# Feed-forward stage of a two-block transformer kernel: the root's product back in the turns, and ScalarE's queue reordered around it

## The reference, cut to what matters

```
h = rms_norm(x, g)                      # x * 1/sqrt(mean(x^2)) * g
gu = h @ w_in                           # 1024 -> 2 * 2816
f = (silu(gu[..., :2816]) * gu[..., 2816:]) @ w_out      # 2816 -> 1024
```

## Time and profile before

| | us |
|---|---|
| median of 3 runs (lowest, highest) | 1759.24 (1759.04, 1760.07) |
| the profiled execution, its own time | 1758.46 |
| span of the profiled execution | 1756.6 |
| matrix engine busy in it | 1684.0 (96%) |
| VectorE, ScalarE, GpSimd busy | 1008.4, 735.9, 678.0 |

### The profile page before, as it was taken

How to read it: one execution, slowest core, us unless ns; L and a number is a source line. 1 busy time by engine, 2 the same in 40 slices (tenths; PEclk the granted TensorE clock), 3 DMA queues, 4 the chain that set the end, 5 groups by cost and what they waited for, 6 DMA issues and landing times.

```text
span 1756.6 us, 25803 instructions
## 1 busy us (share of the span) xinstructions
PE 1684.0 (96%) x8873; PEld 1387.2 (79%) x8877; DVE 1008.4 (57%) x1652; ACT 735.9 (42%) x1187; POOL 678.0 (39%) x308
## 2 busy tenths in 40 slices
PE   9999999999999984999999999999999989996799
PEld 7888777787899974888788766778889879995687
DVE  6744875657767773208497676642234786767113
ACT  7333554434433333327524676542224433333222
POOL 2444222444454423444343003534444344451443
PEclk9999999999999997999999999999999999998899
DMA  5344211222333221234332111122333223331232
GB/s 201 129 146 140 95 61 49 84 88 80 107 98 107 96 96 60 86 106 134 133 96 72 49 49 49 49 83 89 99 101 97 85 83 97 96 103 53 84 97 71
DMA packets 47642, 162.36 MB, mean 92 GB/s; under 512 B 5724, under 2 KB 7900, under 8 KB 47304
## 3 DMA queue, kind: packets, MB, share of 16 engines
q1 hardware_dynamic: 43440, 150.70, 27.1%
q10 hardware_dynamic: 4120, 10.59, 1.8%
HBM read 156.91 MB, written 4.76 MB: 92 GB/s over the span
## 4 chain that ended last, share of the span: by engine, by line
PE 42%; issue 38%; POOL 14%; DVE 3%; ACT 1%; DMA 1%; POOLq 0%; SPq 0%; DVEq 0%; ACTq 0%
POOL w_lo L500 14%; PE ps L584 11%; PE ps L585 11%; PE ps L586 11%; PE ps L1275 1%; PE ps L1274 1%; PE ps L1276 1%; PE ps L824 1%; PE ps L842 1%; PE ps L868 1%; PE ps L1172 1%; PE ps L1131 1%; PE ps L1153 1%; PE ps L1100 1%; DMA hT<-xT 1%
## 5 line engine op out<-in xcount | busy, mean ns | idle before, releaser
L500 POOL TENSOR_TENSOR w_lo<-w_raw,w_hi 128x1024 fp32r<-128x1024 f32 x260 | 638.8, 2463 | 954.1 <-ACT w_hi L1357 927.3
L1357 ACT ACTIVATE w_hi<-w_raw 128x1024 fp32r<-128x1024 f32 x271 | 284.1, 1054 | 350.4 <-PE ps L586 240.5
L584 PE MATMUL ps<-u_hi,w_hi 128*128 128x512 f32 x984 | 403.9, 410 | 6.3 <-POOL w_lo L500 6.1
L586 PE MATMUL ps<-u_hi,w_lo 128*128 128x512 f32 x984 | 385.0, 391 | 0.0
L585 PE MATMUL ps<-u_lo,w_hi 128*128 128x512 f32 x984 | 385.0, 391 | 0.0
L584 PEld LDWEIGHTS ps<-u_hi,w_hi 128*128 128x128 f32 x984 | 185.6, 189 | 51.9 <-issue 8.5
L586 PEld LDWEIGHTS ps<-u_hi,w_lo 128*128 128x128 f32 x984 | 185.3, 188 | 40.0
L585 PEld LDWEIGHTS ps<-u_lo,w_hi 128*128 128x128 f32 x984 | 185.8, 189 | 36.9 <-issue 1.4
L584 PE MATMUL ps<-a_hi,w_hi 128*128 (+1 forms) x264 | 105.0, 398 | 52.1 <-POOL w_lo L500 52.1
L585 PE MATMUL ps<-a_lo,w_hi 128*128 (+1 forms) x264 | 104.2, 395 | 0.0
L586 PE MATMUL ps<-a_hi,w_lo 128*128 (+1 forms) x264 | 104.2, 395 | 0.0
(11 more groups left out here) (455 smaller groups left out, 3594.8 us busy)
## 6 DMA issues: line engine op xcount, KB each, us to landing
w_raw<-stream SPq DMA_DIRECT2D x277, 512.0 KB, 3.5
g_rep<-g_one ACTq DMA_DIRECT2D x1, 2560.0 KB, 14.1
spread<-m_rows ACTq DMA_DIRECT2D x4, 512.0 KB, 4.2
tmp<-tmp ACTq DMA_DIRECT2D x32, 64.0 KB, 2.6
bias<-g_rep ACTq DMA_DIRECT2D x1, 2048.0 KB, 9.3
outT<-hT SPq DMA_DIRECT2D x13, 128.0 KB, 1.8
hT<-xT SPq DMA_DIRECT2D x3, 512.0 KB, 7.4
mem_in<-memT ACTq DMA_DIRECT2D x1, 1024.0 KB, 5.3
```

What stands on the lines that cost most here:

```text
L500: pool.tensor_tensor(w_lo[:, slot], w_raw[:, slot], w_hi[:, slot].bitcast(F32), ALU.subtract)\
L584: pe.matmul(out, wh, xh, start=start, stop=False)
L586: return pe.matmul(out, wl, xh, start=False, stop=stop)
L1357: act.activation(w_hi[:, slot], w_raw[:, slot], ACT.Copy).then_inc(hi_ready, 1)
```

## The change

1. **The root's product goes back into the turns.** `rooted` is gone. `plain_mid` multiplies in place and then by `rs`; `fast_up` has a product by `rs` between its two others. `plain_up` and `fast_up` raise `fast_a` themselves.
2. **The tail on ScalarE.** Eight roundings, feed 8, six roundings, feed 9, the last gate, seven roundings, feed 10 (the third down unit's), the last rounding. `down_act` then no longer feeds that unit, and the memory norm's squares stand behind the feeds of the next six.
3. **The tail on VectorE.** `a_lo` tiles in groups of four between the last gate, mid and up steps.
4. **In a turn on VectorE,** `sums_low(i, 3)` stands before `plain_gate`, not behind it.
5. **The first pairs.** ffn1 on VectorE: all four T tiles first, then the first gate, the weight sums, the rest of the pair, `sums_low`, the second pair. On ScalarE: the feeds of f + 3, f + 4 and f + 5 stand between and behind the T tiles, `sums_hi` before the second gate, and the feeds of f + 6 and f + 7 behind it. ffn2 on VectorE: weight sums ahead of pair 3 and `sums_low` ahead of pair 4; ScalarE's queue to match.

```diff
 # turn(i, last) on ScalarE
-                        for k in range(2):
+                        for k in range(8):
                             split(k)
                         feed_at(i, 8)
-                        for k in range(2, 6):
+                        for k in range(8, 14):
                             split(k)
                         feed_at(i, 9)
                         gate(LAST_E_BANK)
-                        for k in range(6, FT):
+                        for k in range(14, FT - 1):
                             split(k)
+                        feed_at(i, 10)
+                        split(FT - 1)
...
 # down_act
-                feed_after(u)
+                if half:
+                    feed_after(u)
                 if u + 10 + AHEAD < UNITS:
-                    with act.Fori(0, 3) as i:
+                    with act.Fori(0, 2) as i:
                         for j in range(R):
                             feed_loop(u + 1, j, i, R)
+                    if squares:
+                        squares()
+                    for j in range(7, 10):
+                        feed_after(u + j)
...
 # one_turn (ffn1): ScalarE's first turn
                 root("n_ffn", T)
                 feed_after(u + 1)
+                t_tile(2)
+                feed_after(u + 2)
+                t_tile(3)
                 sigmoids()
                 gate()
-                feed_after(u + 2)
-                t_tile(2)
-                t_tile(3)
                 feed_after(u + 3)
+                sums_hi(0, 0)
                 gate()
                 feed_after(u + 4)
-                sums_hi(0, 0)
                 feed_after(u + 5)
                 gate()
...
 # two_turns (ffn2)
                 t_tile(0)
                 t_tile(1)
-                gate()
                 feed_after(u + 8)
-                t_tile(2)
-                t_tile(3)
-                gate()
                 gate()
                 feed_after(u + 9)
+                t_tile(2)
                 feed_after(u + 10)
+                t_tile(3)
                 sums_hi(0, 0)
                 gate()
                 feed_after(u + 11)
+                gate()
+                gate()
...
 # plain_mid on VectorE
-                    step(dve.tensor_tensor(tmp[1][:, :], ps[:, bank, :], tmp[1][:, :], ALU.mult))
+                    x = ps[:, bank, :]
+                    step(dve.tensor_tensor(x, x, tmp[1][:, :], ALU.mult))
+                    step(dve.tensor_tensor(tmp[1][:, :], x, rs[:, :], ALU.mult))
...
 # fast_up on VectorE
                     step(dve.tensor_tensor(x, x, tmp[1][:, :], ALU.mult))
+                    step(dve.tensor_tensor(x, x, rs[:, :], ALU.mult))
                     step(dve.tensor_tensor(a_raw[:, bass.ds(k, 1)], x.unsqueeze(1), late_two[:, :].unsqueeze(1), ALU.mult))
+                    dve.sem_inc(named("fast_a"), 1)
...
 # turn(i, last) on VectorE
                     fast_up(i * R + (k + 1))
-                    plain_gate(i * (2 * R) + (u + 4), ffn2_banks(2)[0])
                     if not last:
                         sums_low(i, 3)
+                    plain_gate(i * (2 * R) + (u + 4), ffn2_banks(2)[0])
                     plain_mid()
...
 # ffn1's first pairs on VectorE
                     two_t_tiles(0)
+                    two_t_tiles(2)
                     dve.wait_ge(*of_norm("n_" + gain, "rs", 1))
-                    pair(0, ffn_banks(0))
-                    two_t_tiles(2)
+                    plain_gate(f, ffn_banks(0)[0])
+                    weight_sums(0, 0)
+                    plain_mid()
+                    plain_up(f + 1, ffn_banks(0)[1], 0)
+                    sums_low(0, 0)
                     pair(1, ffn_banks(1))
 # ffn2's
                     two_t_tiles(2)
+                    weight_sums(0, 0)
                     pair(3, ffn2_banks(0))
+                    sums_low(0, 0)
                     pair(4, ffn2_banks(1))
-                weight_sums(0, 0)
                 plain_gate(u - 2, ffn2_banks(2)[0])
-                sums_low(0, 0)
                 plain_mid()
...
 # the tail on VectorE
-                rooted(0, 2)
+                split(0, 4)
                 plain_up(t - 1, ffn2_banks(2)[1], FT - 2)
-                rooted(2, 6)
-                split(0, 4)
+                split(4, 8)
                 plain_gate(t, ffn2_banks(0)[0])
-                rooted(6, 10)
+                split(8, 12)
                 plain_mid(LAST_E_BANK)
-                split(4, 8)
+                split(12, 14)
                 plain_up(t + 1, ffn2_banks(0)[1], FT - 1)
-                for k in range(10, FT):
-                    rooted(k, k + 1)
-                    split(k - 2, k - 1)
-                split(FT - 2, FT)
+                split(14, FT)
```

More of the change, by code:

```diff
@@ L1826, in memory_split, with down_act @@
                 norm_hi("n_mem", um_hi, MEM)
-            def down_act(name, norm_name, src, half, ahead_of_last=None):
+            def down_act(name, norm_name, src, half, squares=None, ahead_of_last=None):
                 u = FIRST[name]
-                feed_after(u)
+                if half:
+                    feed_after(u)
                 if u + 10 + AHEAD < UNITS:
-                    with act.Fori(0, 3) as i:
+                    with act.Fori(0, 2) as i:
                         for j in range(R):
                             feed_loop(u + 1, j, i, R)
+                    if squares:
+                        squares()
+                    for j in range(7, 10):
+                        feed_after(u + j)
                     if ahead_of_last:
@@ L1865, in _, with memory_squares @@
             ffn_act("ffn1", one_turn, lambda: act.dma_start(mem_in[:], memT).then_inc(loads["mem"], 16))
[L1867 to L1871, removed]
+            def memory_squares():
+                act.wait_ge(loads["mem"], 16)
+                for k in range(KT):
+                    square("n_mem", lambda k: mem_in[:, k], MEM, k)
+            down_act("down1a", "n_fin", lambda k: hT[:, k], 0, memory_squares, memory_split)
             down_act("down1b", "n_fin", lambda k: hT[:, k], 1)
@@ L2637, in split @@
                         dve.sem_inc(named("raw_lo"), 1)
[L2639 to L2643, removed]
                 def turn(i, last):
@@ L2678, in ffn_dve @@
                     two_t_tiles(2)
+                    weight_sums(0, 0)
                     pair(3, ffn2_banks(0))
+                    sums_low(0, 0)
                     pair(4, ffn2_banks(1))
-                weight_sums(0, 0)
                 plain_gate(u - 2, ffn2_banks(2)[0])
-                sums_low(0, 0)
                 plain_mid()
-                with repeat(dve, turns - 1, [(own, 31), (made, 3)]) as i:
+                with repeat(dve, turns - 1, [(own, 34), (made, 3)]) as i:
                     turn(i, False)
```

## The result

| | before | changed |
|---|---|---|
| median (lowest, highest), us | 1759.15 (1759.04, 1760.07), 4 runs | 1729.26 (1728.54, 1729.87), 4 runs |
| span of the profiled execution, us | 1756.6 | 1726.8 |
| ratio to the kernel before, 95% interval | | 0.9829 [0.9812, 0.9846] |

The change takes 29.9 us; 28.4 were forecast, 1731 against 1729.3. In the page the matrix engine is now busy 98% of a shorter span, against 96%; VectorE's 13 us more are mainly the tails' `a_lo` tiles, which now meet `w_lo` more often: 47.1 us in all 44 of them instead of 34.6. `s_lo` adds 2.3, and the products by `rs` take 6 less than before.

A forecast was written before the change was run, and what follows sets the result against it. The matrix engine, 96% busy, idled 72.6 us, 52 in two waits before third down units. Tails -56.6, turns +17, ffn1's start +4.2 and +2.0, ffn2's +4.5 and +0.5 gave -28.4: 1731 us, range 1724 to 1738 (0.55).

The forecast's parts named there:

- The tails, -56.6: Both tails: stalls of 28.09 and 23.99 us before the third down units go, with their half-speed steps: -56.6 us.
- would cost their 4 us once: ffn1's tail: the eight squares cost nothing behind a feed where ScalarE idles; without that cover, 4 us once.
- The turns, +17: Nine turns: `s_lo` loses to `w_lo` by 0.04 us, gate and sigmoid follow it, seventh product waits: 9 x 1.9 = +17 us.
- The rival that VectorE wins: Turns: `s_lo` starts before GpSimd's `w_lo`, old and new waits go: 1731 - 9 x 2.4 = 1709; chance 0.22.
- 2.4 us a turn: Turns: what each of nine would save against the forecast if VectorE won the race, 9 x 2.4 us.
- ffn1's start, +6.2: ffn1's first pairs: waits of 8.7 us in all against 4.5 before, +4.2, and +2.0 for the clock.
- The clock's +2.0: ffn1's first pairs: half-speed steps behind the 5.5 us stall, judged from thirteen (2.5 us) after ffn2's 5.16 us stall.
- ffn2's start, +5.0: ffn2's first pairs: 12.3 us lost against 7.8 before, +4.5, and 0.5 for the clock.
- The fifth product's wait of 2.8 us: ffn2's first pairs: the fifth product waits 2.8 us for ScalarE's copy, which stands behind three sigmoids.
- the +4.5: ffn2's first pairs: 12.3 us for the changed kernel against 7.8 before, which included 2.5 at half clock.

The follow-up runs named there:

- e5: Changed kernel with the root's product still in the turns, but ScalarE's tail in the order of the kernel before, VectorE's `a_lo` groups fitted to it: 1748.01 us.
- e6: Changed kernel with ScalarE's new tail order, but the root's product behind the turns again, in groups ahead of the roundings: 1724.57 us.
- e1: Changed kernel, but in a turn `plain_gate` stands before `sums_low(i, 3)` again; the root's product stays in the turns: 1713.65 us.
- e3: Changed kernel, but the second `fast_up` of a turn raises `fast_a` behind `s_lo` instead of ahead of it: 1707.85 us.
- e12: Kernel before with one line moved, `sums_low(i, 3)` ahead of `plain_gate` (item 4 of the change alone): 1754.32 us.

## Why the prediction was right, step by step

- **The tails, -56.6: measured -56.1** (29.7 + 26.4). The order of feeds and roundings works as reckoned: 0.53 us a rounding, a slack of 6.0 us, no stall, no half clock. e5 and e6 show what this hangs on, and one half of it I had only argued: with the product's place alone (e5) the two tails lose 19.6 us of it, with the order alone (e6) 20.8, so either of them alone brings some 36 of the 56. That the squares "would cost their 4 us once" without cover was mis-sized: 9.1, because they wait for VectorE.
- **The turns, +17: measured +16.7.** The race was lost by 0.05 us in the trace, 0.04 in the sum; the wait in front of the seventh product is 1.65 us idle and 1.9 with the step, as forecast, and `late_sums` releases it. e1 to e3 show it: order and 0.1 us of semaphore work, not the products. The rival that VectorE wins (the first of the list, though the text calls it the second) was a different kernel one line away; its 1709 was e3's 1707.9. "2.4 us a turn" was 2.2 by the spans, since the two steps at the seventh product stay 0.2 us longer. The side it fell on was partly luck: it hung on 0.04 us and a gap of 0.22 us taken from a neighbour, and e3 shows that 0.1 us less there gives 1708.
- **The Trainium skill's rule** ("SBUF - State Buffer", section "Who interferes with whom") that issue order decides who blocks: by that rule, e3's shift of 0.1 us had to turn the stretch from VectorE onto GpSimd, and the traces agree, 3.95 and 2.38 us against 1.76 and 3.97.
- **ffn1's start, +6.2: measured +4.3.** The waits came as 2.33 (2.2 expected) and 4.25 (5.5), 0.2 in front of the seventh product not at all. The prediction's own terms for the waits (2.2, 0.4, 5.5, 0.2) add up to 8.3 and not to its 8.7; the traces' idle time is 6.6. The clock's +2.0 was taken from thirteen long steps at 0.20 us lost each, but behind this wait come short products that lose 0.09 each, twelve of them in this trace: 1.1 us. In e3's trace, with the same two waits of 2.3 and 4.2 us, about twice as many are slow and it is 2.3 us, so this term can't be held against the forecast.
- **ffn2's start, +5.0: measured +4.8, right by two errors.** The fifth product's wait of 2.8 us for ScalarE's copy doesn't exist, and the first and seventh were 0.78 and 2.87 (1.2 and 3.1): 8.2 us of idle time instead of 11.9. But two waits were followed by half clock, about 3.6 us in all (2.5 and 1.1, by the differences to the same matmuls of before). The forecast had only 0.5 for that: its 7.8 us for before hold 2.5 us at half clock, its 12.3 for the changed kernel hold none, so the +4.5 took before's slow steps away and put nothing but the 0.5 in their place. By the same matmuls the changed start costs 12.5 us (12.8 forecast), of which 9.0 are waits with their first steps (12.3 forecast). The waits were 3.3 us too long and the clock 3.1 too short: that they cancel is luck.
- **Not forecast: +0.7** in two norms between the stages, where one step of the matrix engine is 0.4 and one 0.3 us longer; the first of them waits for VectorE's sums. In e6's trace neither is there, and 0.4 us are lost in another place. No run was aimed at it; it stays open.

## What to carry to other kernels

Where two engines share a port and take it for whole instructions, write down both start times before adding anything ahead of the later one: here 0.05 us decided 2.2 us a turn, and moving one semaphore (21.4 us) was worth more than half of what the whole change was (29.9). Put operations that don't need the port (here those that read PSUM) behind the start of the other engine's instruction and those that need it ahead of it. A reordering that gains (item 4, e12) can turn into a loss through a later edit in front of it, so such a line is to be tried again with each of them.

## What was not expected of the hardware

- The race has no middle. Started 0.05 us behind `w_lo`, `s_lo` is 3.95 us long in nine of nine turns; started 0.05 us ahead, 1.76 in nine of nine. 0.05 us is enough in either direction. A blocked instruction isn't shown as waiting: it is recorded as long (3.95 us, with 0.23 us idle ahead of it), and so it looks busy.
- The same idle time in the same place isn't always followed by the same clock. In the changed kernel 2.33 us idle before 434.74 were followed by full clock, in e5 2.31 us before 434.46 by a clock of 0.50, with the same instructions. The windows of e5 and then of the changed kernel:

```profile
435.00:438.00 3.00, 3.00 (x8) 2.35 (x8) 2.56 (x4) 1.49 (x1) 0.00 (x0) 0.50 0.66 175
```

```profile
435.00:438.00 3.00, 3.00 (x14) 2.47 (x14) 2.52 (x5) 1.49 (x1) 0.00 (x0) 1.00 0.55 175
```

Eight matmuls instead of fourteen in 3 us. In e5 this cost nothing in the end: the next wait, for `w_lo`, was 2.62 us instead of 4.25, and the first seventh product starts at 454.65, in the changed kernel at 454.70. But in e1 and e3, which have the changed kernel's first pairs, the steps behind the second wait (5.0 us in e1, 4.2 in e3) stay slow until about 450.2 and 450.5 instead of 447.6, and that product starts at 455.99 and 456.02. So one and the same start came out up to 1.3 us apart, and a forecast of it can't be better than that.
